# Input panels of a second attention layer as three fp32r products instead of one fp32 product

## What is computed

```
k_s, v_s = jnp.split(rmsnorm(x, kv_norm) @ w_kv_shared, 2, axis=-1)
k_shared = rope(rmsnorm(split_heads(k_s, DIL_SLOTS), kv_k_norm), pos)
v_shared = split_heads(v_s, DIL_SLOTS)
q, q_mem = jnp.split(h @ b_w_in[i], [B_Q], axis=-1)        # h = rmsnorm(x, attn_norm[1])
o_main = dilated_attention(q, k_shared, v_shared, b_q_norm[i])
o_mem = memory_attention(q_mem, mem_kv, mem_q_norm[layer], mem_k_norm[layer])
x = x + jnp.concatenate([o_main, o_mem], axis=-1) @ b_w_out[i]
```

## Time and profile before

| | us |
|---|---|
| median of 3 runs | 2197.31 |
| lowest and highest run | 2195.5 and 2214.51 |
| span of the profiled execution | 2196.8 |
| PE busy in it | 2170.1 |
| DVE busy | 1796.1 |
| ACT busy | 1072.4 |
| POOL busy | 27.7 |

### The profile page before, as it was taken

How to read it: one execution, slowest core, us unless ns; L and a number is a source line. 1 busy time by engine, 2 the same in 40 slices (tenths; PEclk the granted TensorE clock), 3 DMA queues, 4 the chain that set the end, 5 groups by cost and what they waited for, 6 DMA issues and landing times.

```text
span 2196.8 us, 40317 instructions
## 1 busy us (share of the span) xinstructions
PE 2170.1 (99%) x15594; PEld 1898.1 (86%) x15594; DVE 1796.1 (82%) x2244; ACT 1072.4 (49%) x1568; POOL 27.7 (1%) x36
## 2 busy tenths in 40 slices
PE   9999999999999999999999999999999999999999
PEld 8999899989999888888888888888888998877998
DVE  6886877778877889898988989898788777678777
ACT  6545400045366578787777878775473000342000
POOL 0000000000000000000000000000000000000000
PEclk9999999999999999999999999999999999999999
DMA  6333467633335799999999999995503555323554
GB/s 255 117 117 123 153 243 238 223 143 134 121 121 180 289 397 387 356 400 348 387 378 370 389 352 400 353 415 211 198 21 124 186 188 191 134 77 115 192 189 155
DMA packets 74118, 514.65 MB, mean 234 GB/s; under 512 B 8224, under 2 KB 8352, under 8 KB 14736
## 3 DMA queue, kind: packets, MB, share of 16 engines
q1 hardware_dynamic: 69552, 493.37, 59.9%
q0 software_dynamic: 4448, 19.59, 2.2%
HBM read 499.29 MB, written 13.63 MB: 233 GB/s over the span
## 4 chain that ended last, share of the span: by engine, by line
PE 88%; DVE 8%; ACT 1%; DMA 1%; issue 1%; SPq 0%; DVEq 0%; ACTq 0%
PE wide L372 30%; PE wide L1290 24%; PE wide L1289 24%; DMA ring<-in_weights 1%; PE wide L1377 1%; DVE ring_lo L2470 1%; PE wide L1079 1%; PE wide L1087 1%; PE wide L1636 1%; PE wide L867 0%; PE wide L1622 0%; PE wide L856 0%; PE wide L1502 0%; ACT p_sb L2262 0%; PE wide L1595 0%
## 5 line engine op out<-in xcount | busy, mean ns | idle before, releaser
L372 PE MATMUL wide<-ring_hi,hT_hi 128*128 128x512 f32 x664 | 262.2, 395 | 0.4 <-DVE ring_lo L3116 0.4
L1290 PE MATMUL wide<-ring_hi,hT_lo 128*128 128x512 f32 x664 | 262.1, 395 | 0.0
L2059 ACT ACTIVATE gate_s<-wide 128x512 f32<-128x512 f32 x43 | 25.8, 599 | 469.8 <-PE wide L1290 469.8
L3010 DVE TENSOR_TENSOR ring_more_lo<-ring_more,ring_hi 128x1024 fp32r<-128x1024 f32 x192 | 225.9, 1222 | 32.9 <-ACT ring_hi L2099 29.0
L372 PE MATMUL wide<-xT_hi,ring_hi 128*128 128x256 f32 x864 | 243.3, 282 | 1.2 <-DVE xT_lo L2458 1.0
L1290 PE MATMUL wide<-xT_hi,ring_lo 128*128 128x256 f32 x864 | 242.8, 281 | 0.0
L1289 PE MATMUL wide<-xT_lo,ring_hi 128*128 128x256 f32 x864 | 242.5, 281 | 0.0
L3010 DVE TENSOR_TENSOR ring_lo<-ring,ring_hi 128x1024 fp32r<-128x1024 f32 x192 | 226.5, 1221 | 18.8 <-ACT ring_hi L2099 16.2
L372 PE MATMUL wide<-mix_xT_hi,mix_hi 128*128 128x256 f32 x816 | 237.7, 291 | 0.1
L1290 PE MATMUL wide<-mix_xT_hi,ring_lo 128*128 128x256 f32 x832 | 233.4, 281 | 0.0
L1289 PE MATMUL wide<-xT_lo,mix_hi 128*128 128x256 f32 x816 | 229.2, 281 | 0.0
(11 more groups left out here) (556 smaller groups left out, 4802.7 us busy)
## 6 DMA issues: line engine op xcount, KB each, us to landing
ring<-in_weights SPq DMA_DIRECT2D x315, 1024.0 KB, 4.9
ring_more<-in_weights SPq DMA_DIRECT2D x120, 1024.0 KB, 6.4
xT<-in_weights SPq DMA_DIRECT2D x24, 1024.0 KB
routed_x<-xe_tm POOLq DMA_DIRECT2D x13, 512.0 KB, 7.0
ln_row<-in_ln_rows POOLq DMA_DIRECT2D x4, 1024.0 KB, 5.2
xe_tm<-routed_x SPq DMA_DIRECT2D x8, 512.0 KB
routed_x<-y_tm SPq DMA_DIRECT2D x7, 512.0 KB, 8.6
x_tm<-in_x SPq DMA_DIRECT2D x2, 512.0 KB, 4.8
```

The costliest lines, as they stand in the source:

```text
L372: ins = self.pe.matmul(out, lhsT, rhs, start=start, stop=stop)
L1290: return pe.matmul(out, lhsT[1], rhs[0], start=False, stop=stop)
L2059: act.activation(gate_s[:, slot, :, :], b[:].rearrange("p (m t) -> p m t", m=2), func).then_inc(sems["out"], 1)
L3010: tt_(lo[:, c], w[:, c], panel_hi(k)[:, c].bitcast(F32), ALU.subtract).then_inc(S["panel_split"], 1)
```

## The change

- All eleven panels are taken in two parts. ACT writes the high part in two halves (`widen_b`), into three places by turns (`b_panel`). POOL, which had nothing to do in this stage, subtracts it from the panel in place, also by halves (two inputs in SBUF, 128x1024), and gives `branch_or_b_lo`. PE waits for that by halves and makes three fp32r products (`project_half`).
- x is split for both gains by `split_xT`: high part by ACT, low part by DVE. The pair for keys and values is `xT_hi, xT_lo`, that for queries is `q_hi, in_lo`. For the queries, ACT's list has `widen_b(2)` before the split, and PE waits for all four parts of it before panel 2.
- ACT's list has `widen_b(j)` between the copies out, the roots and the turned heads.
- Buffers are laid out anew (`xT_hi` beside `xT_lo` for the whole kernel, `q_hi` over `gate_s` and `hT`, the compression's tiles as one), and counts of `x_split` are shifted. `root(1)` writes its unused squares to `o_tm` instead of `p_sb`. No other instruction changes.

In the diff `project_half` is PE's, `widen_b` and the long list are ACT's, the two `split_xT` after it are DVE's, and the last loop is POOL's.

```diff
+def b_panel(j):
+    n = ORDER.index((B_ORDER[0][0], 1, B_ORDER[0][1])) - AFTER_MOE + j
+    hi = (p_sb_lo[:].rearrange("p a b -> p (a b)")[:, 0:PANEL], cmp_all_r[:, 0:PANEL], ring_hi[:, 0, :])[j % 3]
+    return n, (BEFORE_MOE + n) % RING, hi
...
+def project_half(j, tt):
+    n = PANELS_ATTN[0] + j
+    if tt == 0:
+        panels.held = b_panel(j)[2], ring_lo[:, panels.step(), :]
+        pe.wait_ge(S["attn_read"], n - 1)
+    kv = B_ORDER[j][0] == "kv"
+    for kb in range(KB):
+        if tt == 0 and kb % (KB // 2) == 0:
+            pe.wait_ge(S["branch_or_b_lo"], N_BRANCH * DEPTH + 2 * j + kb // (KB // 2) + 1)
+        if j == 0 and tt == 0 and kb % 2 == 0:
+            pe.wait_ge(S["x_split"], 4 * 5 + kb // 2 + 1)
+        x_ = [t[:, kb, tt * P:(tt + 1) * P] for t in ((xT_hi, xT_lo) if kv else (q_hi, in_lo))]
+        ins = mm3(bank[4 + n % 2][:, tt * PC:(tt + 1) * PC], x_, [t[:, kb * PC:(kb + 1) * PC] for t in panels.held],
+                  start=(kb == 0), stop=(kb == KB - 1))
...
-                    project_tokens(2, n_proj, turn=n_turn)
-                    wait_xT(n_turn + 1)
-                    project_tokens(2, n_proj + 2, xT2)
+                    project_split(0, 1)
+                    pe.wait_ge(S["x_split"], 4 * 7)
+                    project_split(2, 3)
                     turn_heads(1, 2, (9, 6, 7))
-                    project_tokens(2, n_proj + 4, xT2)
+                    project_split(4, 5)
                     turn_heads(1, 3, (0, 1))
-                    project_tokens(2, n_proj + 6, xT2)
+                    project_split(6, 7)
                     turn_heads(1, 4, (2, 3))
...
+def widen_b(j):
+    n, slot, hi = b_panel(j)
+    act.wait_ge(landed_2[slot], 16 * (n // RING + 1))
+    if j >= 3:
+        act.wait_ge(S["panel_used_2"], n - 2)
+    for half in range(2):
+        c = slice(half * PANEL // 2, (half + 1) * PANEL // 2)
+        act.activation(hi[:, c], ring[:, slot, c], ACT.Copy).then_inc(S["attn_hi"], 1)
...
-                    copy_xT(n_turn, "kv_norm")
-                    copy_xT(n_turn + 1, "attn_norm1", dst=xT2)
+                    widen_b(0)
+                    widen_b(1)
+                    split_xT(n_turn, xT_hi, "kv_norm")
+                    widen_b(2)
+                    split_xT(n_turn + 1, q_hi, "attn_norm1")
                     root(1)
                     head_std(1, 0)
                     panel(0)
+                    widen_b(3)
                     panel(1)
+                    widen_b(4)
                     head_std(1, 1)
                     panel(2)
+                    widen_b(5)
                     panel(3)
+                    widen_b(6)
                     turned_heads((9, 6, 7))
                     head_std(1, 2)
                     panel(4)
+                    widen_b(7)
                     panel(5)
+                    widen_b(8)
                     turned_heads((0, 1))
                     head_std(1, 3)
                     panel(6)
+                    widen_b(9)
                     panel(7)
+                    widen_b(10)
                     turned_heads((2, 3))
                     head_std(1, 4)
...
-                    copy_xT(n_turn, "kv_norm")
-                    copy_xT(n_turn + 1, "attn_norm1", dst=xT2)
+                    split_xT(n_turn, xT_hi, "kv_norm")
+                    split_xT(n_turn + 1, q_hi, "attn_norm1", lo=in_lo)
...
+            for j in range(PANELS_ATTN[1]):
+                _, slot, hi = b_panel(j)
+                for half in range(2):
+                    c = slice(half * PANEL // 2, (half + 1) * PANEL // 2)
+                    pool.wait_ge(S["attn_hi"], IN_SPLITS + 1 + 2 * j + half + 1)
+                    pool.tensor_tensor(ring_lo[:, slot, c], ring[:, slot, c], hi[:, c].bitcast(F32), ALU.subtract).then_inc(S["branch_or_b_lo"], 1)
```

More of the change, by code:

```diff
@@ L561, in program @@
         rs = sb("rs", 416, stack=attn)
[L562 to L566, removed]
+        cmp_all, cmp_all_r = twice_named("cmp_all", 1440 + 180 + 2 * 384, stack=attn)
+        cmp_in = cmp_all[:, 0:1440].rearrange("p (k l g i) -> p k l g i", k=2, l=CMP_BLOCK // 2, g=NSA_G)
+        cmp_h = cmp_all[:, 1440:1620].rearrange("p (k h n) -> p k h n", k=2, h=2)
+        cmp_kv = cmp_all[:, 1620:2004].rearrange("p (k g e) -> p k g e", k=2, g=NSA_G)
+        cmp_dup = cmp_all[:, 2004:2388].rearrange("p (g d e) -> p g d e", g=NSA_G, d=2)
         cmp_kT = sb("cmp_kT", NSA_G, 16, stack=attn)
@@ L932, in project @@
                         pe.wait_ge(S["x_split"], 4 * (2 * l) + kb // 2 + 1)
-                    ins = mm3(bank[n % 2][:, m * T:(m + 1) * T], [t[:, kb * PC + m * P:][:, 0:P] for t in w], (mix_xT_hi[:, kb, :], xT_lo[:, kb, :]),
+                    ins = mm3(bank[n % 2][:, m * T:(m + 1) * T], [t[:, kb * PC + m * P:][:, 0:P] for t in w], (xT_hi[:, kb, :], xT_lo[:, kb, :]),
                               start=(kb == 0 and (m == 0 or i > 0)), stop=(kb == KB - 1 and (m == 1 or i > 0)))
@@ L1490, in project_short, with project_split @@
                 ins.then_inc(S["attn_proj"], 1)
+            def project_half(j, tt):
[12 more added lines that the diff above has]
+                              start=(kb == 0), stop=(kb == KB - 1))
+                if tt == TT - 1:
+                    ins.then_inc(S["attn_proj"], 1)
+            def project_split(*js):
+                for j in js:
+                    for tt in range(TT):
+                        project_half(j, tt)
             def turn_heads(l, ready, groups, into=None):
@@ L2202, in root @@
                     act.wait_ge(S["ln_x_done"], 2 * DEPTH)
-                squares(p_sb).then_inc(S["act_step"], 1)
+                squares((p_sb, o_tm)[l]).then_inc(S["act_step"], 1)
                 act.wait_ge(S["act_step"], made.next("act_step"))
@@ L2443, in copy_xT, with split_xT @@
                     dve.wait_ge(S["xT_dve"], made.next("xT_dve"))
-            def split_xT(n, hi, gain=None, bias=None):
+            def split_xT(n, hi, gain=None, bias=None, lo=xT_lo):
                 for b in range(4):
@@ L2457, in split_xT @@
                         for f in (2 * b, 2 * b + 1):
-                            ins = stt(xT_lo[:, f, :], turn_bank(n, b)[:, f % 2 * T:][:, 0:T], c1(gain, f), hi[:, f, :].bitcast(F32), ALU.mult, ALU.subtract)
+                            ins = stt(lo[:, f, :], turn_bank(n, b)[:, f % 2 * T:][:, 0:T], c1(gain, f), hi[:, f, :].bitcast(F32), ALU.mult, ALU.subtract)
                     else:
-                        ins = tt_(xT_lo[:, fs, :], pair(turn_bank(n, b)) if gain is None else xT[:, fs, :], hi[:, fs, :].bitcast(F32), ALU.subtract)
+                        ins = tt_(lo[:, fs, :], pair(turn_bank(n, b)) if gain is None else xT[:, fs, :], hi[:, fs, :].bitcast(F32), ALU.subtract)
                     ins.then_inc(S["x_split"], 1)
```

55 lines of the change are left out of this document (27 added, 28 removed).

## The result

The changed kernel took 2249.53 us in the median of 4 runs (2240.85 to 2260.52), the kernel before 2199.11 beside it (4 runs). The ratio is 1.0229, with an interval of 1.0198 to 1.0261. The forecast was 2235, within 2210 to 2250.

What follows compares the result with a forecast made beforehand. PE bounds the kernel, but the chain through ACT and DVE is nearly as long; 17.0 (chain) - 1.5 (panel 10's halves) + 18.7 (exclusion) + 4 (clock) = 38.2 on 2196.8 gives 2235.0 us, range 2210 to 2250.

Steps and rivals of the forecast that it cites:

- The price of a panel on PE: PE's panel products: 5.66 us as three fp32r products against 6.91 now, 1.25 less each, 13.8 for eleven.
- Panel 2: Start of the stage: panel 2 waits behind ACT's list and starts at 1889.9 instead of 1883.7, a stall of over 7 us.
- The loop through ACT's list: Query pairs: load, high part, turned heads, root and norm take 18.1, 17.6, 17.6 us; panel 10 starts 17.0 later.
- The prediction's rival without exclusion: POOL's and DVE's reads do not shut each other out: all but the 18.7 us stands, 2216; chance 0.28.
- The exclusion: Norms beside POOL's subtractions: only one engine reads SBUF at a time, costing 3.4, 6.7, 6.7 and 1.9 us, 18.7; chance 0.50.
- POOL's price: POOL's subtraction in the stage: 2.4 us a half, 4.8 a panel, between ends of 1.94 and 2.91 a half.
- The keys: Norm and turn of the keys: panel 4 starts at 1906.7 instead of 1898.97, plus 3.4 us from POOL's panel 4.
- The start: PE's first matmul of the stage: the split of x puts it at 1871.0, 1.2 us later than now.
- The clock in the stage: After the new stalls PE runs at the lower clock and transposes double, 3.9 us, taken as 4.
- POOL over 2.91 a half: Rival on POOL's subtraction: each us more a half adds 12; 2254 at 4.0; chance 0.12.
- The gain comes through: Rival: PE stays the bound, 13.8 us less and 1.2 more at the start, 2184; chance 0.05.
- A short loop: Rival on the pairs: an earlier load or root shortens the loop and panel gains make up for most, 2200 to 2210; chance 0.05.

Runs made afterwards that it cites:

- e3_order_no_read: Changed kernel with high parts moved later in ACT's list and POOL writing zeros by memset instead of low parts; 2190.86 us median, ratio 0.9973.
- the second sample: The changed kernel run and profiled once more, with no edit; 2247.53 us median of 4 runs, ratio 1.0219.
- e1_order: Changed kernel with each `widen_b` moved in ACT's list behind the copy of a panel, POOL as in the change; 2219.53 to 2235.38 us, ratio 1.0123.
- e2_no_read: Changed kernel, ACT's list kept, low parts left out and two POOL memsets in place of each subtraction; 2217.72 to 2238.39 us, ratio 1.0145.
- e6_pool_copy: Changed kernel with POOL copying the high part, one input read instead of two, low parts left out; 2225.95 us in one execution.
- e4_busy: Changed kernel with unread matmuls on PE before panel 2 and before turns of heads; 2241.34 to 2254.40 us, ratio 1.0237.
- e7_kv_only: Changed kernel cut to panels 0, 1, 9 and 10 in two parts, queries as before the change; 2199.65 us median, ratio 1.0017.
- e5_dve_low: Changed kernel with ACT's list as in e1_order and all eleven low parts by DVE instead of POOL; 2205.63 us median, ratio 1.0023.
- e8_mixed: Like e7_kv_only, but panels 5 and 7 also in two parts and ACT's list in order of need; 2193.67 us median, ratio 0.9958.

## Why the prediction was right, and where its terms were off

The mechanism was right: a loop through ACT's list, made longer by exclusion. The number was helped by luck. The median of 2249.53 lies 0.5 inside the end of the range and 14.5 above 2235, and 9 of these come from the clock's drop behind the stage, which no step had. Two of the four runs have it; with a third the median would have been over 2254. Without the drop the time is 2240.6.

**What bounds the kernel** stood: PE was the bound with slacks of 2.1 and 3.5, and the change put more than that into the chain beside it. In the norms of the keys and of the queries alone PE lost 34.9 us.

**The price of a panel on PE, 5.66**, held. In e3_order_no_read, where nothing holds PE, a pair takes 12.22, 11.3 of it for two panels. The gain was real and lay off the path that sets the end.

**Panel 2**, forecast 18.9 after the first matmul, came at 18.4, 18.6 in the second sample. In e1_order, with `widen_b(2)` behind the root, it came at 14.4.

**The loop through ACT's list**, forecast 18.1, 17.6 and 17.6 without exclusion, and 19.0, 18.5 and 18.5 with the transposes at the lower clock, is what e2_no_read shows: 18.5, 18.5 and 18.1. The prediction's rival without exclusion gave 2216, and this kernel takes 2217.7 or 2218.7.

**The exclusion** was the step I gave one chance in two. It holds: the norms got 5.7, 6.2 and 2.0 longer against 6.7, 6.7 and 1.9 forecast. Pairs of 24.7, 24.3 and 20.4 stand against 25.7, 25.2 and 20.4, which is 24.8, 24.3 and 19.5 and 0.87 each for the lower clock. The rule of the Trainium skill (SBUF — State Buffer, section Who interferes with whom) is that a VectorE instruction with two SBUF inputs contends with a GpSimd instruction that reads SBUF, and the trace agrees: 0.69 becomes 2.1 to 2.8 beside POOL's 2.38. An instruction of DVE with one input from PSUM beside POOL's subtraction kept its 3.4 for eight, and `TENSOR_REDUCE` its 0.69.

**POOL's price**, taken at 2.4 a half from a memset at 0.97, measured 2.38 where nothing holds it (4.75 to 4.78 for two) and up to 2.7 where DVE does. That the middle was hit is luck. The picture behind it was one stream after another at 0.97 each, and it does not hold: POOL's copy in e6_pool_copy has two streams and takes 1.02, the subtraction has three and takes 2.38. The page GPSIMD Engine Reference of the Trainium skill (section 3.1) led to an estimate of 2.25, half of its 4497 ns; the measurement decides.

**Four things were mis-sized.**
- The keys. "It costs 3.4 at the keys" counted POOL's panel 4 only. Its panel 5 comes in the same norm, since the norm is by then late enough (POOL 5.38 from 1908.14, DVE's instructions of 2.72 and 2.71 from 1908.61). The norm took 14.2, from 1901.99 to 1916.20, and not 10.8. A piece of work that is lengthened by an overlap reaches the next overlap: it has to be laid out again after the first is added.
- The start, 2.3 and not 1.2. The load of panel 1 took 6.05 (chain of waits) and not the median of 4.8, and its high part stands ahead of the split in ACT's list: it began at 1871.73, 1.1 after the turning of x, and the forecast had it begin 0.2 before.
- The clock in the stage. "I take 4" was laid to the transposes, which did double (1.97 for 0.87, 2.82 for 1.31: 4.8 in the table above). The first half of panel 10 began at the lower level too, and takes 3.74 where the sum had 3.46 less 0.63, 0.9 more.
- The clock behind the stage, 17 us in this profile, in some executions. No step of the prediction had it.

Up to the scores the profile is 42.3 us longer than before (2.3 + 4.5 + 9.8 + 25.4 + 0.3). The sum had 39.0 there; 0.8 of its gain, the second half of panel 10, lies behind. The parts are off both ways: the start 1.1 over, panel 2 0.5 under, the keys with their turn 3.6 over, the three pairs with theirs 1.7 under (mainly since two norms grew by 5.7 and 6.2 and not by 6.7), the half panel 0.9 over. So part of the closeness is errors that cancel. The lower times of the runs are 43.2 above before, and the whole sum was 38.2.

**The rivals.** POOL over 2.91 a half: no, 2.38. The gain comes through: no, but e3_order_no_read says what it wanted, both edits at once. A short loop: no.

**What stays open** is what brings on the lower clock behind the stage. By their times it was there in 4 of 8 runs of the changed kernel, 1 of 4 of e1_order, 2 of 4 of e2_no_read, 3 of 4 of e4_busy, 2 of 12 of e3_order_no_read, 4 of 12 of e7_kv_only, and in none of the ten of e5_dve_low and of the twelve of e8_mixed. The kernel before, whose stage has no stall, has it in 12 of 57. So idle time in the stage is not needed for it, as e4_busy says too. That it came in 7 of 16 runs of the kernels that stall there may mean that the stalls make it likelier, or it may be chance; no run separates the two.

## What to carry to other kernels

When an engine with nothing to do is given work on SBUF, ask first which instructions of the other engine run at that time and whether they read two inputs from there: the free engine cost 22 us here, and the busy one did the same work in half the time. When a load is put into an in-order list, ask what stands behind it: a wait for the next panel ahead of a root that was ready turned slack into a loop of load, copy, root and norm, and moving it behind a wait that had to be kept anyway gave half of the loss back. And when a cheaper product is bought with work elsewhere, buy only as many as the other engines' time in one turn of the loop allows: eleven panels lost 43 us here, and six of them gained 4.

## What the runs showed of the hardware

- POOL's copy with one input of 128x1024 (1.02 us) keeps DVE's instructions with two SBUF inputs waiting just as its subtraction does (0.76 became 2.42 for two). Its memset of the same size (0.95 us) does not. I had thought of the subtraction's two reads.
- DVE subtracts 128x1024 from SBUF in 1.18 us (2.36 for two), POOL in 2.38.
- The granted clock fell to 0.50 for 30 to 44 us in the middle of an attention stage in which PE was busy for 95 to 100% of the time, in some executions of a kernel and not in others; from the scores to the first panel out it cost 12 to 17 us in the three profiles that have it.
